# A decoder kernel's normalisations: blocks scaled two pairs ahead of their rounding

## What is computed

```
h2 = _modulate(_rms_norm(x, norm2_g[l]), shift2, scale2)      # norm 0, before the feed-forward part
...
return _rms_norm(x, final_g)                                  # norm 1, before the hybrid layers
...
out = (zf - mu) * lax.rsqrt(var + LN_EPS) * g + b             # norm 2 after hybrid layer 0, norm 3 after layer 1
```

## Time and profile before

| | |
|---|---|
| median of 3 runs | 2897.89 us (2897.39 to 2899.75) |
| profiled execution, its own time | 2899.83 us |
| its span | 2898.0 us |
| TensorE busy | 2756.3 us, 95% |
| VectorE busy | 1877.8 us, 65% |
| ScalarE busy | 1393.1 us, 48% |
| Pool busy | 329.6 us, 11% |
| HBM read | 573.01 MB, 198 GB/s over the span |

### The profile page before, as it was taken

One profiled execution on the slowest core, in us unless ns is written; L12 is line 12 of the kernel. 1 busy time (PEld: TensorE's weight loads), 2 busy tenths in 40 slices (PEclk: granted clock), 3 DMA queues, 4 the chain that ended last, 5 costly groups with the idle time before them and its releaser, 6 DMA issues.

```text
span 2898.0 us, 52927 instructions
## 1 busy us (share of the span) xinstructions
PE 2756.3 (95%) x22458; PEld 2705.9 (93%) x22458; DVE 1877.8 (65%) x2295; ACT 1393.1 (48%) x1989; POOL 329.6 (11%) x265
## 2 busy tenths in 40 slices
PE   2699999999999899999999998999999989999997
PEld 1699899999999799999999998999999989999997
DVE  7877887776787765555555555566465665664655
ACT  1255566665545554444444444444554444445543
POOL 2010122222323220000000000100010111000001
PEclk6799999999999999999999999999999999999998
DMA  9854577777788675555555554555445645554453
GB/s 340 324 196 156 176 251 233 237 258 260 274 281 301 221 269 182 182 183 183 184 185 182 182 175 150 177 188 170 159 146 176 205 153 172 185 175 157 145 170 111
DMA packets 161866, 583.84 MB, mean 201 GB/s; under 512 B 19008, under 2 KB 20288, under 8 KB 161504
## 3 DMA queue, kind: packets, MB, share of 16 engines
q1 hardware_dynamic: 156816, 565.82, 58.4%
q0 software_dynamic: 4528, 12.43, 1.4%
q10 hardware_dynamic: 288, 2.23, 0.2%
HBM read 573.01 MB, written 2.15 MB: 198 GB/s over the span
## 4 chain that ended last, share of the span: by engine, by line
PE 61%; DVE 2%; ACT 1%; issue 0%; ACTq 0%; DVEq 0%
PE bank L684 18%; PE bank L685 17%; PE bank L686 17%; PE bank L692 2%; PE bank L693 2%; PE bank L694 2%; DVE wlo L1317 1%; PE pO L750 1%; PE pS L727 1%; ACT whi L946 1%; PE pS L780 1%; PE pT L739 0%; PE pM L792 0%; ACT Hhi L1118 0%; ACT RES L1129 0%
## 5 line engine op out<-in xcount | busy, mean ns | idle before, releaser
L1317 DVE TENSOR_TENSOR wlo<-raw,whi 128x1024 fp32r<-128x1024 f32 (+1 forms) x880 | 1152.1, 1319 | 755.2 <-ACT whi L946 753.8
L946 ACT ACTIVATE whi<-raw 128x1024 fp32r<-128x1024 f32 (+1 forms) x880 | 920.5, 1050 | 721.0 <-PE bank L686 626.7
L684 PE MATMUL bank<-Hhi,whi 128*128 128x256 f32 x4128 | 1186.3, 287 | 27.2 <-DVE Hlo L1606 11.8
L685 PE MATMUL bank<-Hlo,whi 128*128 128x256 f32 x4128 | 1172.9, 284 | 0.0
L686 PE MATMUL bank<-Hhi,wlo 128*128 128x256 f32 x4128 | 1172.6, 284 | 0.0
L684 PEld LDWEIGHTS bank<-Hhi,whi 128*128 128x128 f32 x4128 | 796.9, 193 | 39.3 <-issue 11.2
L685 PEld LDWEIGHTS bank<-Hlo,whi 128*128 128x128 f32 x4128 | 797.3, 193 | 0.6
L686 PEld LDWEIGHTS bank<-Hhi,wlo 128*128 128x128 f32 x4128 | 797.0, 193 | 0.0
L684 PE MATMUL bank<-Fh,whi 128*128 128x256 f32 x1024 | 289.8, 283 | 0.0
L685 PE MATMUL bank<-Fl,whi 128*128 128x256 f32 x1024 | 289.8, 283 | 0.0
L686 PE MATMUL bank<-Fh,wlo 128*128 128x256 f32 x1024 | 289.8, 283 | 0.0
(11 more groups left out here) (308 smaller groups left out, 3616.5 us busy)
## 6 DMA issues: line engine op xcount, KB each, us to landing
raw<-in_w_in SPq DMA_DIRECT2D x424, 512.0 KB, 3.7
raw<-in_w_ff SPq DMA_DIRECT2D x256, 512.0 KB, 3.8
raw<-in_ada SPq DMA_DIRECT2D x192, 512.0 KB, 5.0
raw<-in_w_out SPq DMA_DIRECT2D x96, 512.0 KB, 4.3
raw<-in_w_lru_out SPq DMA_DIRECT2D x32, 512.0 KB, 4.8
raw<-in_w_attn_out SPq DMA_DIRECT2D x32, 512.0 KB, 5.0
raw<-in_w_kv SPq DMA_DIRECT2D x32, 512.0 KB, 4.6
BT<-gtab POOLq DMA_DIRECT2D x32, 128.0 KB, 4.0
```

Of the source, the lines that this page charges most:

```text
L684: pe.matmul(o, h, xh[:, kt, :], start=start, stop=False, skip_group_check=True)
L685: pe.matmul(o, h, xl[:, kt, :], start=False, stop=False, skip_group_check=True)
L946: act.activation(whi[:, s, 0:el.n], raw[el.slot][:, 0:el.n], ACT.Copy).then_inc(s_hi, 1)
L1317: dve.tensor_tensor(wlo[:, s, 0:n], raw[el.slot][:, 0:n], v32(whi[:, s, 0:n]), ALU.subtract).then_inc(s_lo, 1)
```

## The change

VectorE's `blocks` now scales pairs 0 and 1 at once, in the tick of the Newton step. In each of the next eight ticks it writes `Hlo` of pair q and then scales pair q+2. Its scaling into a used slot waits on `s_h`, its own count of `Hlo` written. ScalarE and Pool start with pair 0 in the tick in which they get there, since their `yield` has moved behind the pair. Norm 3 isn't touched, and no instruction is added or removed.

```diff
         def blocks(n, kind):
 
             for q in range(8):
-                yield
                 for b in (2 * q, 2 * q + 1):
                     act.wait_ge(s_sl, 16 * n + b + 1)
...
                     ins.then_inc(s_hh, 1)
+                yield
...
         def blocks(n, kind, gain, shift):
 
-            for q in range(9):
+
+
+            def scaled(q):
+                for b in (2 * q, 2 * q + 1):
+                    if kind != "rms" and b >= 4:
+
+                        dve.wait_ge(s_h, 20 + 16 * n + b - 3)
+                        if kind == "ln":
+                            dve.wait_ge(s_hp, b - 3)
+                    dst = RES[:, b, :] if kind == "rms" else tslot(b)
+                    dve.scalar_tensor_tensor(out=dst, in0=RES[:, b, :], scalar=gain(b), in1=Rv, op0=ALU.mult,
+                                             op1=ALU.mult).then_inc(s_sl, 1)
+
+            scaled(0)
+            scaled(1)
+            for q in range(8):
                 yield
-                for b in (2 * q - 2, 2 * q - 1):
-                    if q:
-                        dve.wait_ge(s_hh, 16 * (n + 1) + b + 1)
...
                 for b in (2 * q, 2 * q + 1):
-                    if q < 8:
-                        if kind == "ln" and b >= 4:
-                            dve.wait_ge(s_hp, b - 3)
...
+                    dve.wait_ge(s_hh, 16 * (n + 1) + b + 1)
...
+                    ins.then_inc(s_h, 1)
+                if q < 6:
+                    scaled(q + 2)
...
                 for q in range(8):
-                    yield
                     for b in (2 * q, 2 * q + 1):
                         pool.wait_ge(s_sl, 32 + b + 1)
                         pool.tensor_scalar(RES[:, b, :], tslot(b), ones[:, 0:1], v(V_LNB + b), ALU.mult, ALU.add).then_inc(s_hp, 1)
+                    yield
```

More of the change, by code:

```diff
@@ L1116, in blocks @@
                         ins = act.activation(Hhi[:, b, :], RES[:, b, :], ACT.Copy)
-                    elif kind == "ln":
+                    else:
                         ins = act.activation(Hhi[:, b, :], tslot(b), ACT.Identity, bias=v(V_LNB + b))
                     ins.then_inc(s_hh, 1)
+                yield
         def norm(n):
@@ L1596, in blocks @@
         def blocks(n, kind, gain, shift):
-            for q in range(9):
-                yield
-                for b in (2 * q - 2, 2 * q - 1):
-                    if q:
-                        dve.wait_ge(s_hh, 16 * (n + 1) + b + 1)
[L1603 to L1608, removed]
-                for b in (2 * q, 2 * q + 1):
-                    if q < 8:
-                        if kind == "ln" and b >= 4:
-                            dve.wait_ge(s_hp, b - 3)
-                        dst = RES[:, b, :] if kind == "rms" else tslot(b)
-                        dve.scalar_tensor_tensor(out=dst, in0=RES[:, b, :], scalar=gain(b), in1=Rv, op0=ALU.mult,
-                                                 op1=ALU.mult).then_inc(s_sl, 1)
+            def scaled(q):
[7 more added lines that the diff above has]
+                                             op1=ALU.mult).then_inc(s_sl, 1)
@@ new lines, in blocks @@
+            scaled(0)
+            scaled(1)
+            for q in range(8):
+                yield
+                for b in (2 * q, 2 * q + 1):
+                    dve.wait_ge(s_hh, 16 * (n + 1) + b + 1)
+                    if kind == "rms":
+                        ins = dve.tensor_tensor(Hlo[:, b, :], RES[:, b, :], v32(Hhi[:, b, :]), ALU.subtract)
+                    else:
+                        ins = dve.scalar_tensor_tensor(out=Hlo[:, b, :], in0=tslot(b), scalar=shift(b), in1=v32(Hhi[:, b, :]),
+                                                       op0=ALU.add, op1=ALU.subtract)
+                    ins.then_inc(s_h, 1)
+                if q < 6:
+                    scaled(q + 2)
```

## The result

| | before | with the change |
|---|---|---|
| median | 2898.23 us, 4 runs (2897.39 to 2899.75) | 2867.62 us, 4 runs (2867.04 to 2868.40) |
| profiled execution, its own time | 2899.83 us | 2867.29 us |
| its span | 2898.0 us | 2865.5 us |

The ratio is 0.9894, with a 95% interval of 0.9882 to 0.9907: the kernel is 30.6 us faster. The forecast was 2868.9 us, in a range of 2861 to 2880; it was right, in its size too.

The account below looks back on a forecast made before the run. TensorE's 28.8 us of waits in three normalisation stretches, caused by a serial VectorE and ScalarE chain, were taken as the bound. Gains of 15.0 + 10.0 + 4.0 = 29.0 us from 2897.89 gave 2868.9 us, range 2861 to 2880.

Parts of the forecast that it names:

- What bounds the kernel: TensorE waits 28.8 us in three normalisation stretches, on a serial VectorE and ScalarE chain of 4.34 us per tick.
- Scaling ahead: Blocks of norms 0 to 2: scaling two pairs ahead lets both engines overlap; tick 2.72 us, under TensorE's 2.88 us.
- One tick earlier: `Hlo` moves one tick earlier, taking 4.34 us of lateness off its wait in norms 0 and 1, nothing in norm 2.
- The entry of norm 0: Next weights stand behind the Newton step and Pool's add holds their split: `wlo` ready at 979.4 us, 1.4 us late.
- The rest of norm 0: After the entry, one further wait of about 1 us at the last chunk; norm 0 gains 15.0 us in all.
- My lower end: Norm 0's gain is 11 us in place of 15.0 if Pool's adds fall badly twice more.
- Norm 1: Second normalisation: waits of 7.9 us, slow clock of 1.8 us and restarts all go; 10.0 us gained, ends 7.5 and 10.5.
- Norm 2: Third normalisation: 4.0 us gained, between 3.7 if Pool's pass fully blocks VectorE and 8 if not; entry wait 1.0 us.
- Nothing takes turns: Rival, chance 0.10: VectorE and Pool don't meet, TensorE waits only at two entries; 34 us gained, 2864 us.
- The entry costs the clock: Rival, chance 0.07: new waits entering norms 0 and 2 each lower the clock; 16 us gained, 2882 us.
- Paced by TensorE: Rival, chance 0.03: ScalarE's weights already wait for TensorE to free buffers, so a shorter chain changes nothing; 2898 us.
- Slower: Rival, chance 0.02: ticks stay at 4.34 us or longer, so late entry weights cost 7.7 us; 2906 us.

Follow-up runs that it names:

- the first experiment: Changed kernel, but VectorE scales only one pair ahead, behind `Hlo` of the current pair; ScalarE and Pool still start early: 2896.79 us, ratio 0.9992.
- third experiments: Changed kernel, but ScalarE and Pool start one tick later and VectorE scales one pair ahead, in front of `Hlo`: 2866.60 us, ratio 0.9887.
- the second experiment: Changed kernel, but ScalarE and Pool start one tick later, as before the change; VectorE still scales two pairs ahead: 2868.72 us, ratio 0.9894.
- fourth experiment: Changed kernel, but Pool's pass in norm 2 handles one column in place of 256: 2868.66 us, ratio 0.9892.
- the change once more: The changed kernel itself, unaltered, measured again on the second chip as a reference: 2868.35 us, ratio 0.9896.
- norm 0 only: Changed kernel with the new blocks only in norm 0; norms 1 and 2 use the loops from before: 2885.08 us, ratio 0.9957.

## Why the prediction was right, and where its terms were off

**What bounds the kernel** held. The share of waits read from the earlier trace rows was the right ceiling: 30.8 us came out of 28.8 us of waits, 5.7 us of slow clock and some restarts, with 5.8 us of waits left. That the serial chain of the earlier trace rows is the cause, the first and third experiments show.

**Scaling ahead.** The tick was worked out as 2.72 us for VectorE, and 2.72 us is what the rows have. The new wait `s_h` costs nothing, as said: VectorE's waits in the three stretches are for ScalarE's weights and in the Newton steps, none before a scaling. In norm 1 the tick is even 2.60 us, since `Hlo` on line 1618 is an operation of 0.75 us a pair; I had used norm 0's for it.

**One tick earlier.** I gave it 4.34 us of lateness in the first two stretches. It isn't needed for that: the second experiment starts ScalarE a tick later and norm 1's stretch is the same 543.15 us. And alone, in the first experiment, it gives 0.4 and 2.9 us. Once the tick is under TensorE's 2.88 us the lead isn't eaten, and a tick of start is worth nothing. With it, in norm 0, the stretch up to the last wait is even 1.2 us longer, by the entry's wait. This step was argued wrongly, but no term of the sum stood on it alone.

**The entry of norm 0.** It went as worked out. The Newton instruction took 0.43 us in place of 2.53, Pool's add then held the split, `wlo` was ready at 977.87 us (979.4 was forecast, 977.7 if the stretch's start 1.7 us earlier is taken off), and the wait was 1.35 us for 1.4.

**The rest of norm 0** is the step that failed: "find one further wait of about 1 us at the last chunk", with only "another add of Pool". Two adds came, at 992.07 and 999.22 us, and each held an `Hlo` pair by 2.1 to 2.2 us, so the further waits were 0.39 + 3.46 = 3.85 us, 2.85 more than forecast; the sign "TensorE's waits for `Hlo` below 2 us in the first" failed. That is why the term was 12.9 us and not 15.0; the 0.7 us by which it is better than 15.0 - 2.85 are left by difference. My lower end, 11 "if Pool's adds fall badly twice more", was this case. That the slow clock's 3.9 us came back in full was in part luck: the forecast inferred it from waits of up to 1.4 us, the wait became 3.46 us, and behind that wait the clock fell in three profiles out of six, for 1.4 to 2.6 us. The two experiments on the adds take the same waits away, once by moving and once by emptying them.

**Norm 1** was 10.8 us for 10.0, 0.3 over the upper end that I gave it. The waits (7.9 us) and the slow clock (1.8) are all gone, and its window shows TensorE busy without a gap. The other 1.1 us are left by difference; that they are what restarts cost in the kernel before is argued, not measured.

**Norm 2** was the other mis-sized term: 7.2 us for 4.0. I took Pool's whole pass, 1.1 us in each tick, as lost to VectorE, "since that collision was total". Measured it is 0.36 us (fourth experiment). The rule of the Trainium skill ("SBUF — State Buffer", Who interferes with whom), that whoever comes second blocks fully, held for the long adds of norm 0: the split at 975.29 and the two `Hlo` pairs ended only after the add beside them. In norm 2 the rows don't follow it: the split at 2305.23 starts after Pool's pair (2305.01) and takes 1.21 us, as it does alone. Which engine holds the other there no row shows, and the low price stays without a cause. "VectorE waiting for Pool" by `s_hp`, which I named as a sign, wasn't seen in the changed kernel. The entry's wait was 0.64 us for 1.0. From before to after the waits fell by 7.5 - 0.6 = 6.9 us; the rest of the 7.2 is left by difference.

**The rivals.** *Nothing takes turns* is refuted in norm 0 (3.05 us pairs) and by the 0.36 us per tick in norm 2, though it came close there. *The entry costs the clock*: no; the waits at the entries, 1.35 and 0.64 us, left it at 1.00. What can cost it is the later wait of 3.46 us, which this rival didn't name. *Paced by TensorE* as I meant it would have made the change worthless; it didn't, but it is what the kernel has become in norm 1. *Slower* needed ticks of 4.34 us. The first experiment had ticks of 4.12 to 4.34 us with the late entry and came out at 0.9992, not 8 us slower: the earlier start and the late entry about cancel. By stretches the rival's mechanism is there: norm 2, where `wlo` comes last, lost 2.0 us (2.7 were forecast for that entry), while norms 0 and 1, where `Hlo` is still waited for, lost nothing. So its premise that `wlo` would come last in all three didn't hold.

The sum hit to 1.3 us (1.8 by the stretches, 30.8 against 29.0) because errors of -2.1, +0.8 and +3.2 us partly cancelled, which is luck. The right mechanism, and three terms with bounds, carried it; the single terms are to be trusted no further than those.

## What to carry to other kernels

In code where in-order engines hand pieces to each other once per tick, look for a piece that waits for another engine's work of the same tick: the tick is then nearly the sum of both engines' work and not the larger. One step of distance suffices (ticks of 4.12 against 2.60 us in norm 1, by the same arithmetic), and starting earlier doesn't replace it. Once VectorE has little to spare, the next thing to look at is any Pool instruction of some length in that stretch: moving Pool's adds past it took away 4.2 us of waits, and the risk of a slow clock behind them, and made the best kernel here, 2860.47 us. And where one stretch of a profile is longer than the same code elsewhere, look at its granted clock before looking for a cause in the kernel.

## What the runs showed of the hardware that was not expected

- **What Pool costs VectorE isn't Pool's time.** Against one add of Pool of 128 x 1024 (2.4 us) VectorE was held for up to nearly the whole of it: a pair of 0.87 us became 3.05. Against Pool instructions of 128 x 256 it lost 0.36 us per two of them. Pool's rows were twice as long there as beside a VectorE that mostly stood still (2.72 for 1.26 us a pair), with 256 columns and with one.
- **The granted clock** didn't follow from the longest wait alone. A wait of 4.9 us was followed by the level of 1.2 GHz in the kernel before. One of 3.46 to 3.47 us at the same place was followed by it in three profiles (the second, third and fourth experiment: means of 0.70, 0.84 and 0.83 over the next 10 us) and not in three others (the change, the change once more, and norm 0 only: 1.00), and four of these six have the same code in norm 0. From there to norm 1's cut it took 733.50 us with the change and 736.13, 734.86 and 734.98 where the clock had fallen. Waits of up to 2.5 us, four in all, brought it down in norm 1 before. The first experiment had five there, of up to 2.4 us and 6.7 in total, and its clock stayed at 1.00, while in norm 0 its waits of up to 4.2 us did bring it down. These are the two windows of it:

```profile
1006.00:1013.00 7.00, 2.51 (x13) 2.25 (x14) 6.67 (x9) 4.79 (x6) 2.34 (x1) 0.59 0.82 252
1782.00:1792.00 10.00, 7.25 (x58) 7.08 (x59) 7.14 (x11) 5.69 (x8) 0.00 (x0) 1.00 0.28 73
```

  What decides was not tried by itself and stays open.
- **Scatter has a place, and it is mostly the clock.** The way to norm 0 varied by 3.5 us over ten profiles; the two that arrive last (966.44 and 966.92 us) are the two with a clock of 0.93 from 648 to 672 us, where the other eight have 1.00. Norm 0's stretch varied by 1.5 us with the same code, by the clock behind the wait of 3.46 us, and norm 1's, where no clock fell, by 0.03 us. The 1.35 us of Pool's pass in norm 2 can be seen in its stretch and not in the whole time.
